# The input convolution's projections of a state-space block, as seven half products for eight

## The reference, cut to what matters

```python
h = rmsnorm(x, norm1_w) * (1 + sc1) + sh1          # 512 tokens, and the same for 256 context tokens
p = h @ w_in                                        # 1024 -> x: 2048, B: 512+512, C: 512+512, dt, z: 2048, ...
xl = silu(dwconv_centred(p[..., :XB_CH], conv_w, conv_b))        # 5 taps along the tokens, per channel
cl = silu(dwconv_centred(p[..., OFF_CF:OFF_Z], conv_w, conv_b))
# then per head group: states of four chunks of 128 tokens, forward and backward, and
y = y_f + y_b + d_skip * xs
y_ssd = rmsnorm(y * silu(z), ssd_norm_w) @ w_ssd_out
```

## Time and profile before

| what | value |
|---|---|
| median of 3 runs | 3127.45 us (3127.22 to 3131.87) |
| the profiled execution | 3125.53 us, of which its span is 3123.6 us |
| mean granted TensorE clock of that execution | 0.985 |
| state-space groups 1 and 2, first product to first product | 184.91 to 322.38, and 322.38 to 459.86 |

### The profile page before, as it was taken

One profiled execution on the slowest core, in us unless ns is written; L12 is line 12 of the kernel. 1 busy time (PEld: TensorE's weight loads), 2 busy tenths in 40 slices (PEclk: granted clock), 3 DMA queues, 4 the chain that ended last, 5 costly groups with the idle time before them and its releaser, 6 DMA issues.

```text
span 3123.6 us, 43848 instructions
## 1 busy us (share of the span) xinstructions
PE 2995.2 (96%) x15990; PEld 1790.3 (57%) x15991; DVE 1324.4 (42%) x2223; ACT 865.6 (28%) x1698; POOL 353.2 (11%) x337
## 2 busy tenths in 40 slices
PE   8999999999999899998999969998999999999999
PEld 4555655655888333332333313333887888888887
DVE  4555464744355222221222212222675677454552
ACT  4445363610212121221222211221434455211100
POOL 0202011521001000000000000001211453000000
PEclk9999999999999899999999989999999999999999
DMA  5414323346124799879999698999220221122121
GB/s 218 154 66 145 128 95 128 146 155 215 54 82 174 307 400 408 325 303 405 395 392 398 233 406 335 395 399 348 90 112 1 80 86 74 59 87 81 54 81 57
DMA packets 137462, 630.21 MB, mean 202 GB/s; under 512 B 14256, under 2 KB 55088, under 8 KB 77200
## 3 DMA queue, kind: packets, MB, share of 16 engines
q1 hardware_dynamic: 106896, 554.16, 45.4%
q0 software_dynamic: 10896, 38.41, 3.8%
q10 hardware_dynamic: 19568, 36.21, 3.3%
HBM read 593.47 MB, written 35.26 MB: 201 GB/s over the span
## 4 chain that ended last, share of the span: by engine, by line
PE 85%; DMA 5%; DVE 4%; ACT 2%; issue 2%; POOL 1%; SPq 1%; ACTq 0%; DVEq 0%; another core or an unknown queue 0%; POOLq 0%
PE ps L330 25%; PE ps L2450 19%; PE ps L2422 10%; PE ps L2091 10%; PE ps L279 6%; DMA slot<-in_w_exp 4%; PE ps L2185 2%; PE ps L2703 2%; PE ps L2194 2%; PE ps L2675 1%; PE ps L2413 1%; PE ps L2408 1%; PE ps L2658 1%; DMA slot<-in_w_mod 1%; PE ps L2632 1%
## 5 line engine op out<-in xcount | busy, mean ns | idle before, releaser
L2450 PE MATMUL ps<-slot,xT_blk 128*32 128x512 f32 (+1 forms) x3840 | 673.6, 611 | 74.6 <-DMA slot<-in_w_exp 72.8
L2450 PEld LDWEIGHTS ps<-slot,xT_blk 128*32 128x32 f32 (+1 forms) x3840 | 184.0, 125 | 471.5 <-issue 364.8
L2422 PE MATMUL ps<-slot,aT 128*32 128x256 f32 (+1 forms) x2912 | 331.1, 455 | 0.0
L2091 PE MATMUL ps<-hT,slot 128*128 128x512 f32 (+1 forms) x896 | 308.1, 501 | 0.0
L3239 DVE TENSOR_TENSOR gate<-ps,b_row 128x256 f32<-128x256 f32 (+1 forms) x60 | 33.5, 558 | 510.7 <-PE ps L2450 510.7
L2422 PEld LDWEIGHTS ps<-slot,aT 128*32 128x32 f32 (+1 forms) x2912 | 128.1, 119 | 212.0 <-issue 175.9
L2091 PEld LDWEIGHTS ps<-hT,slot 128*128 128x128 f32 x896 | 167.9, 190 | 128.5 <-issue 119.7
L2839 DVE SCALAR_TENSOR_TENSOR conv<-ps,g_conv,conv 128x510 f32<-128x510 f32 (+1 forms) x224 | 133.3, 631 | 170.2 <-ACT conv L1561 166.8
L3235 DVE MEMSET b_there<- 128x1 f32 x60 | 3.5, 59 | 359.4 <-DMA b_few<-in_b_gu 344.2
L1755 ACT ACTIVATE y_row<-ps 128x512 f32<-128x512 f32 (+1 forms) x61 | 30.0, 492 | 393.1 <-PE ps L2422 393.1
L330 PE MATMUL ps<-in_t,in_s 128*128 128x264 f32 x528 | 124.7, 386 | 0.5 <-issue 0.5
(11 more groups left out here) (518 smaller groups left out, 4663.3 us busy)
## 6 DMA issues: line engine op xcount, KB each, us to landing
slot<-in_w_exp SPq DMA_DIRECT2D x384, 1024.0 KB, 9.1
in_w<-in_w_ffn SPq DMA_DIRECT2D x22, 1024.0 KB, 4.8
expert_rows<-zero SPq DMA_DIRECT2D x4, 4608.0 KB, 24.8
slot<-in_w_xbc SPq DMA_DIRECT2D x8, 2048.0 KB, 7.7
sum_here<-sum_rows ACTq DMA_DIRECT2D x32, 512.0 KB, 3.6
w_modT<-in_w_modT POOLq DMA_DIRECT2D x32, 512.0 KB, 3.8
rnn_w<-in_w_rnn SPq DMA_DIRECT2D x16, 1024.0 KB, 4.8
out_w<-in_w_ffn_out SPq DMA_DIRECT2D x8, 1408.0 KB, 8.7
```

The costliest lines, as they stand in the source:

```text
L2091: last = pe.matmul(ps[:, 2 * (m % 2) + part, 0:n], w[:, (k * 4 + m % 4) * P:(k * 4 + m % 4 + 1) * P], hT[:, k, c0:c0 + n], start=(k == 0), ...
L2422: last = pe.matmul(ps[j * rows:(j + 1) * rows, Y_BANK_OF[s], 0:width], aT[s][:, 2 * half + c, tile * rows:(tile + 1) * rows], slot[4 + k / ...
L2450: last = pe.matmul(GATE_PS[s][tile * rows:(tile + 1) * rows, half, :], xT_blk[:, k, first:first + rows], slot[i // 4][:, at:at + 512], sta ...
```

## The change

The eight tiles become four pairs (0,1), (2,3), (4,5), (6,7). Blocks of 128 columns are taken alternately as token half 0 and half 1, so a pair has two halves of 384 columns (the last pair of 256). Each pair is computed in seven products p1 to p7, each over 4 of the `k` tiles. Four need a weight sum (`w_sum`, DVE, 512 elements each), four an activation sum (`h_sum`, DVE, once at the start). ACT copies the running sum out of PSUM four times a pair (first11, first12, first22, done21) into `raw`, four SBUF tiles; DVE adds three times (done11, done22, done12). Centre and taps now read `raw`, so that the taps have both inputs in SBUF. The tiles of a pair are taken in the order 1, 0, 3, 2, 5, 4, 7, 6, with the odd one first. z0 is cut into four quarters that stand between the last pair's products. DVE, ACT and SP have their loop over groups written out. `raw` and `conv_b` lie over `decay` and `c_into`, `w_sum` over `state`, `h_sum` in `gate_yT`; so `gate_yT` holds one group, and finished groups go to DRAM (`y_rows`, 1 MB each) and come back (3 MB) during the last one. DVE builds the next group's first weight sums between masked7 and y0.

The diff, cut to its core:

```diff
+    TILE_ORDER = [1, 0, 3, 2, 5, 4, 7, 6]
+    TOP_BANK, SUM_BANK = [0, 1], [3, 2]
+    def window(i):
+        more = i + 1 < 4
+        turned = [f"turned{2 * i - 1}"] if i else [], [f"turned{2 * i - 2}"] if i else []
+        if more:
+            return ([f"p6_{i}", f"p1_{i + 1}", f"p7_{i}"] + turned[0] + [f"p5_{i + 1}", f"p4_{i}", f"p3_{i}"] + turned[1] + [f"p2_{i + 1}"])
+        return [f"p6_{i}", f"p7_{i}", f"p4_{i}", f"p3_{i}"] + turned[0] + turned[1]
...
+    def pair_weight(g, i, r, c):
+        w = slot[SSD_SLOT[g % 2, "ab"[i // 2]][0]][:].rearrange("p (k m c) -> p k m c", k=KD, m=4)
+        return w[:, c * (KD // 2):(c + 1) * (KD // 2), 2 * (i % 2) + r, :]
...
         # SP
+            load_ssd("a", io["w_xbc"], 2 * g)
+            if g:
+                ssd_pe.after(sp, "z3", g - 1)
+            load_ssd("b", io["w_xbc"], 2 * g + 1)
+            if g:
+                ssd_dve.after(sp, "gated3", g - 1)
+                sp.dma_start(y_rows[g - 1], gate_yT[:, 0:4, :]...).then_inc(s_y_out, 16)
+            ssd_pe.after(sp, "p4_1", g)
+            conv_sums.after(sp, "s4_1", g)
+            load_ssd("z", io["w_z"], g)
...
         # ACT, per group
+            for i in range(3):
+                if i or g:
+                    quarter_out(g, i, "first12", "p6", 0, 1)
+                if i:
+                    silu(2 * i - 1)
+                quarter_out(g, i, "first22", "p7", 1, 1)
+                if i:
+                    silu(2 * i - 2)
+                quarter_out(g, i + 1, "first11", "p1", 0, 0)
+                quarter_out(g, i, "done21", "p4", 1, 0)
+                centre(2 * i + 1)
+                if i:
+                    token(2 * i - 1)
+                centre(2 * i)
+                if i:
+                    token(2 * i - 2)
+            quarter_out(g, 3, "first12", "p6", 0, 1)
+            silu(5)
+            quarter_out(g, 3, "first22", "p7", 1, 1)
+            silu(4)
+            quarter_out(g, 3, "done21", "p4", 1, 0)
+            centre(7)
+            centre(6)
+            token(5)
+            silu(7)
+            token(4)
+            silu(6)
...
         # PE
+        def p3(g, i):
+            conv_sums.after(pe, f"s4_{i}", g)
+            ssd_dve.after(pe, f"done22_{i}", g)
...
-            z_piece(0, 0, 1)
+            p6(g, 3)
+            z_piece(0, 0, 4)
+            p7(g, 3)
+            z_piece(0, 1, 4)
+            p4(g, 3)
+            z_piece(0, 2, 4)
+            p3(g, 3)
+            turn_tile(5)
+            turn_tile(4)
+            z_piece(0, 3, 4)
             states(0, [0, 1])       # now waits for token4, before for token5
             scores(0)               # now waits for silu6, before for silu7
...
         # DVE, per group
+            for i in range(4):
+                more = i + 1 < 4
+                if i or g:
+                    added_11(g, i)
+                    if more:
+                        weight_sum(g, 1, i + 1)
+                tap(2 * i - 1, TAPS[2:])
+                if more and (i or g):
+                    weight_sum(g, 2, i + 1)
+                tap(2 * i - 2, TAPS[:2])
+                added_22(g, i)
+                if more:
+                    weight_sum(g, 3, i + 1)
+                tap(2 * i - 2, TAPS[2:])
+                tap(2 * i + 1, TAPS[:2])
+                added_12(g, i)
+                if more:
+                    weight_sum(g, 4, i + 1)
+            tap(7, TAPS[2:])
+            tap(6, TAPS)
...
+                        last = dve.scalar_tensor_tensor(
+                            out=acc[:, lo:hi], in0=raw_tile(m)[:, lo + off:hi + off],
+                            scalar=g_conv[:, m, k:k + 1], in1=acc[:, lo:hi], op0=ALU.mult, op1=ALU.add)
...
         # POOL
-            ssd_act.after(pool, "token3", g)
-            ssd_dve.after(pool, "g_skip", g)
+            ssd_act.after(pool, "token2", g)
+            ssd_dve.after(pool, "g_small", g)
             x_end_(0)
             x_dt_(0)
```

More of the change, by code:

```diff
@@ L676, in program @@
     ssd_act = Steps(sem("ssd_act"),
-                    [n for m in range(8) for n in ([f"centre{m}", f"silu{m}"] + ([f"token{m - 1}"] if 1 <= m < 7 else []))]
+                    ["first11_0"]
+                    + [n for i in range(3) for n in
+                       [f"first12_{i}"] + ([f"silu{2 * i - 1}"] if i else []) + [f"first22_{i}"] + ([f"silu{2 * i - 2}"] if i else [])
+                       + [f"first11_{i + 1}", f"done21_{i}", f"centre{2 * i + 1}"] + ([f"token{2 * i - 1}"] if i else [])
+                       + [f"centre{2 * i}"] + ([f"token{2 * i - 2}"] if i else [])]
+                    + ["first12_3", "silu5", "first22_3", "silu4", "done21_3", "centre7", "centre6", "token5", "silu7", "token4", "silu6"]
                     + ["into0", "apart0", "z0", "decay0", "into1", "apart1", "decay1"]
@@ L1528, in _, with quarter_out @@
         dt_act.done(act.activation(dt_head[:, SEQ:W1], ps[:, DT_HEAD_BANK + 1, 0:CTX], ACT.Copy), "head")
+        ssd_act.open(act)
+        def quarter_out(g, i, name, step, r, l):
+            ssd_pe.after(act, f"{step}_{i}", g)
+            if name == "first11" and i == 0 and g:
+                ssd_pe.after(act, "diagonal7", g - 1)
+            elif name == "first11" and i >= 2:
+                ssd_dve.after(act, f"tap{2 * i - 4}_4", g)
+            ssd_act.done(act.activation(raw_half(2 * i + r, l), above(i, pair_blocks(i)), ACT.Copy), f"{name}_{i}")
+        quarter_out(0, 0, "first11", "p1", 0, 0)
         dt_dve.after(act, "raw")
@@ L1538, in _ @@
         dt_act.done(act.activation(small[:, OVER], over_psum, ACT.Exp), "over")
-        ssd_act.open(act)
-        with act.Fori(0, GROUPS) as g:
+        for g in range(GROUPS):
             def load_sums(j):
@@ L2085, in _, with pair_product @@
         dt_pair(3)
[L2087 to L2092, removed]
-            return last
-        pe.wait_ge(*ssd_weights(0, 0, "a"))
-        conv_product(0, 0, 0, range(1))
+        def pair_product(out, left, right, start):
+            for k in range(KD // 2):
+                last = pe.matmul(out, left[:, k, :], right(k), start=(start and k == 0), stop=(k == KD // 2 - 1), skip_group_check=not start)
+            return last
@@ L2165, in states @@
                     elif i == 0:
-                        ssd_dve.after(pe, "state0_4" if d else "tap6_4", g)
+                        ssd_dve.after(pe, "state0_4" if d else "done11_3", g)
+                    elif d == 0:
+                        ssd_act.after(pe, "done21_3", g)
                     ssd_pe.done(pe.matmul(ps[:, i % 2, :], b_tok[:, t, d, :], x_end[:, end_tile(d, t), :], start=True, stop=True),
@@ L2174, in scores @@
                 else:
-                    ssd_act.after(pe, "silu7", g)
+                    ssd_act.after(pe, "silu6", g)
                 tokens = slice(t * P, (t + 1) * P)
@@ L2869, in weigh @@
                 if j == 0:
-                    ssd_act.after(dve, "silu7", g)
+                    ssd_act.after(dve, "silu6", g)
                 ssd_act.after(dve, f"into{j}", g)
@@ L3590, in h_quarter @@
             return quarter(hT, c, l)
-        ssd_pe.after(pool, "conv7", GROUPS - 1)
+        ssd_pe.after(pool, "p3_3", GROUPS - 1)
         f_in.sum_x1(pool, h_quarter)
```

373 lines of the change are left out of this document (268 added, 105 removed).

## The result

| what | before | after |
|---|---|---|
| median (6 runs each) | 3128.47 us (3127.22 to 3131.87) | 3138.62 us (3136.64 to 3142.23) |
| the profiled execution | 3125.53 us, span 3123.6 | 3137.93 us, span 3136.1 |
| mean granted TensorE clock | 0.985 | 0.976 |

The ratio is 1.0038, interval 1.0027 to 1.0049: 10 us slower, where 16.7 were forecast. It lies inside the range and on the side named as likeliest.

The account below looks back on a forecast made before the run. The state-space stage was taken as bound by PE (136.57 of 137 us a group). -37.5 - 1.8 + 4 x 12.5 + 4 x 1.5 = +16.7 us on 3127.45 gave 3144 us, range 3108 to 3156.

Parts of the forecast that it names:

- The products: Convolution on PE: seven half products replace each pair's full ones, gaining 9.37 us a group, 37.5 us over four.
- Rival (5): Products: 384 strided columns cost more than their share, 3152 us at 3% more; chance 0.13 together with another rival.
- The start: Stage start: the stall before the first transposes goes, activation sums mostly covered; gain 1.8 us (0.3 to 1.8).
- The steady windows: Windows of the pairs before the tail: DVE and ACT work fits beside PE's 19.4 us; cost 0.
- Rival (4): Steady windows starve too, 1 us each over 12 windows, 3156 us; chance 0.13 together with another rival.
- The end of the convolution: From p6_3 to state0_4: DVE and ACT's chain ends 5.1 us behind PE in every group; bounds 3.5 to 6.5.
- POOL beside the taps: Taps of tiles 5 and 4: POOL's x_end and x_dt hold DVE up 7.5 us a group; bounds 3 and 8.7.
- Rivals (1) and (3): State-space: POOL and taps hardly hurt each other, 3108.5 us, chance 0.19; products do all they can, 3088 us, chance 0.04.
- The clock: Each convolution tail: PE's waits lower its granted clock, losing 1.5 us a group; bounds 0 and 3.
- The sum: Whole kernel: gains of 37.5 and 1.8 against losses of 12.5 and 1.5 a group give +16.7 us, 3144 us.
- rival (2): Convolution tail: lag near 9 to 10 us with little clock loss, -3 to +4 us, 3127 us; chance 0.14.
- The signs named: Tail: right if PE waits some 10 us or more, x_end takes 8 us or more, a group lasts about 142 us.

Follow-up runs that it names:

- a_all: Changed kernel with x_dt behind the last tap, z0's copy before silu6, state steps 2 and 3 before masked0, x_end in two halves; 3102.21 us, ratio 0.9911.
- a_narrow: Changed kernel with POOL's first x_end and x_dt of each group cut to 8 columns of 512; totals not comparable, stage ends 19.4 us earlier.
- a_late: Changed kernel with only POOL's first-direction x_dt made to wait for the last tap; 3125.52 us, ratio 0.9991.
- a_late_z_st: Changed kernel with x_dt behind the last tap, z0's copy before silu6, state steps 2 and 3 before masked0; 3111.76 us, ratio 0.9941.

## Why the prediction was right, point by point

- **The products, -9.37 us a group.** Held. Timeline of PE of the kernel after in the steady part: a half product of 384 columns follows the last by 2.58 us (203.49, 206.06, 208.65), one of 256 by 1.73 (247.41, 249.14). Rival (5) is out. With a_all the gain shows itself: its groups take 130.57 us where 137.48 - 9.37 = 128.1 would be possible.
- **The start, -1.8 us.** Held: the wait of the earlier trace rows is gone, and PE has no wait from 40.62 to 119.71, so the activation sums ahead of the dt steps (1.76 us each, as estimated from the width) cost nothing. Group 0's state0_4 stands 0.84 us later than before; with its lag of 12.1 and the two gains that is accounted for to 0.1 us.
- **The steady windows, 0.** Held. All waits of PE above 0.25 us stand in the four tails or in the last group's scan, where the kernel before has the same three, and no window of pairs 0 to 2 has any. Rival (4) is out.
- **The end of the convolution, 5.1 us.** Right in kind, 0.7 too large: 4.4 by a_narrow without its slow z1. The chain was the one that I had followed as far as apart0: silu4, centre7 behind it on ACT, the taps of tiles 7 and 6, silu6, the table load. From there it went through the copy of z0 and the half of z1, and not through decay0 and state step 2.
- **POOL beside the taps, 7.5 us.** 7.3 measured on DVE, 6.3 on the path: in a_narrow the second four of taps ran into a wait of 0.57 us for ACT that POOL's slowdown had covered. Rivals (1) and (3) fall with this term. The extrapolation from c_into and the recurrence's taps to these taps was the step that decided the sign, and it held to within a tenth: 0.78 us an instruction of 1.0 us, against 0.84 from the earlier trace rows, and 3.4 of 3.6 us for the long one. One reading on the way there was wrong: `x_end` of the kernel before hardly ran beside tile 5's taps. It ends at 251.72, DVE had stood idle until the taps began at 251.11, and only `x_dt` lies whole beside them. That `x_dt` alone shows that taps reading PSUM weren't held up (4.66 us, as tile 4's without POOL), and it was enough.
- **The clock, 1.5 us.** 1.7 (the half of z1, 5.28 for 3.60). Its other 3.2 us, on p3_3 and the states, are each followed by a wait for ACT, so they aren't on the path in this kernel.
- **The sum.** Lag and clock were to be 14.0 us a group, and are 12.1 in group 0 and 12.3 to 12.4 in the others. The scan behind state0_4 to the next group is another 0.4 us shorter (42.90 for 43.32 us; 0.2 in the last group), an alignment that I had put at nothing. 49.1 - 1.5 = 47.6, less 39.3 is the +8.3 of the ledger, where 56.0 stood for +16.7. So the error is in size, in the lag of 12.5: its two parts were counted one behind the other, and they overlap by about one us, and the base was 0.7 too large. The stage's +8.3 lies about midway between the forecast and rival (2), -3 to +4 us; against that rival stands the lag itself, 12.4 and not 9 to 10. The other 1.9 us between the two medians arise outside this stage; that they bring the time nearer to the forecast is chance.
- **The signs named.** x_end "8 us or more" was wrong: it took 6.3, and still the taps beside it went from 0.6 to 1.0 and 2.0 us on average (3.99 / 4 and 7.91 / 4). POOL and DVE wait for each other in turns here, so neither duration alone shows the loss. The waits of PE in a group were 7.3 us and not over 10, since 4.9 us of the lag are slow instructions. And the last wait was for ACT's copy of z0, which stands in no step of the prediction; state step 2, which does, was ready only 1.6 us before state0_4 ran. A group was 140.1 us, for 142. Neither sign of being wrong came.

The rule of the Trainium skill that stands in the prediction (SBUF — State Buffer, "Who interferes with whom": a lock held for a whole instruction) agrees with the traces of the kernel after and a_late: one tap instruction of 255 columns lasts 3.83 us beside `x_dt` and 0.47 where `x_dt` is moved away. The figure of 8.7 us by the rule alone was too high, because five short instructions of POOL alternate with five tap instructions, and each of those loses 0.7 to 0.9 us where POOL's last 1.0 undisturbed.

**What stays open.** Why the part behind the stage varies by up to 7 us between these kernels. Whether the base lag of 4.4 us comes from z0 being spent between the last products, or only from the two tiles of taps behind them: a kernel with z0 whole behind p3_3 wasn't tried. And what is left in a_all: 5.7 us of waits in front of the states, 5.1 for decay, 4.8 for c_into, over four groups.

## What to carry to other kernels

Before moving an operand from PSUM to SBUF, look at what POOL does at that hour: here a DVE instruction with two SBUF inputs lost about 0.8 us to each POOL instruction of 1.0 us and 3.4 to one of 3.6. The long one could be released a few steps later, and half of the short ones' work a few steps earlier, at almost no cost. Where work is taken from the engine that bounds, follow the chain to the next stage's first product through every engine: what was hidden there can come out at its full length, and slow PE work behind the waits comes on top. When two waits end at nearly the same time, edits tried one by one show nothing (+1.0 and 0.0 us) and together a lot (9.1 us beyond the 14.0 of a_late).

## What was not expected of the hardware

The clock after a wait can't be told from the wait's length. In one execution of a_late_z_st the first states wait about equally long in groups 0, 1 and 2, and run at half speed in two of them:

```profile
129.67 3.75 PE L2354 MATMUL ps<-x_end,b_tok 128*128 128x512 f32 x4 [3.27 <-issue]
...
395.75 3.75 PE L2354 MATMUL ps<-x_end,b_tok 128*128 128x512 f32 x4 [3.36 <-issue]
```

Group 1's row stands above: 1.95 us after a wait of 3.37. From state0_4 to state0_4 it is 131.43 us into group 1 and 134.72 into group 2; 2.2 of these 3.3 us are the lag (3.75 and 6.0), the rest lies in group 1's scan, which then waited 0.8 us for decay. In windows of the kernel after, the granted clock (third last column) is below full in each of four windows around the waits, so that PE ran part of each at the lower of its two levels (1.2 GHz of 2.4), and is full right after:

```profile
257.00:263.00 6.00, 3.54 (x9) 2.26 (x8) 5.42 (x6) 0.51 (x1) 2.61 (x1) 0.76 0.93 352
263.00:269.00 6.00, 3.92 (x19) 2.39 (x17) 4.35 (x7) 3.98 (x9) 0.00 (x0) 0.96 0.00 0
269.00:277.00 8.00, 5.58 (x10) 2.36 (x10) 4.52 (x7) 5.88 (x14) 0.00 (x0) 0.79 0.00 0
277.00:283.00 6.00, 5.63 (x10) 2.46 (x10) 4.50 (x6) 5.60 (x12) 0.00 (x0) 0.72 0.29 107
283.00:290.00 7.00, 7.00 (x52) 3.90 (x52) 6.12 (x6) 4.63 (x12) 6.40 (x4) 1.00 0.22 81
```

The Trainium skill (TensorE: Matmul & The Clock Gate, "What's actually happening") says that the windows in which activity is judged run freely and aren't started by the kernel's work. The two outcomes in one execution agree with that, but no run here isolates it.
